# A two-block transformer kernel: expert rows gathered one by one, each with its own wait and its index from the routing's tile

## What is computed

```
eidx = i1 * 128 + i2                       # (tokens, 8, 16) chosen experts
g    = softmax(scores of the chosen)
act  = gelu(sum_d x[t, d] * u[eidx][d])
out[t] = sum over the 128 chosen of g * act * v[eidx]
```

## The kernel before, in words

| block | window in the trace, us | goal | issued before | issued after |
|---|---|---|---|---|
| project, half 1 | 767 to 1024 | 140 | 144 | 156 |
| scan | to 1182 | 200 | 208 | 216 |
| merge | to 1541 | 372 | 384 | 388 |
| norm of the expert layer | to 1580 | 384 | 400 | 400 |
| route | to 1845 | 512 | 512 | 512 |
| final norm, half 0 (next 512 slots) | to 1877 | 10 | 16 | 26 |
| norm of layer two | to 1916 | 24 | 32 | 40 |
| project_two | to 2062 | 110 | 112 | 126 |
| latent_heads | to 2167 | 154 | 160 | 170 |
| attend | to 2389 | 262 | 272 | 278 |
| merge_two | to 2510 | 326 | 336 | 342 |
| norm_add | to 2549 | 338 | 352 | 354 |
| norm of the MLP | to 2589 | 354 | 368 | 370 |
| mlp | to 2869 | 512 | 512 | 512 |

## Time and profile before

### The profile page before, as it was taken

How to read it: one execution, slowest core, us unless ns; L and a number is a source line. 1 busy time by engine, 2 the same in 40 slices (tenths; PEclk the granted TensorE clock), 3 DMA queues, 4 the chain that set the end, 5 groups by cost and what they waited for, 6 DMA issues and landing times. The chain is left out here.

```text
span 3440.3 us, 27636 instructions
## 1 busy us (share of the span) xinstructions
PE 2261.2 (66%) x8920; PEld 1658.5 (48%) x8920; DVE 1935.4 (56%) x3625; ACT 486.0 (14%) x1247; POOL 1348.0 (39%) x1232
## 2 busy tenths in 40 slices
PE   7976999808865488765462642134507993988898
PEld 5745887706625376644321531012306642755763
DVE  3327011588969758655997577685946664061100
ACT  3412100203212100001011001011011101131210
POOL 0000000007765676643565767685746752000000
PEclk9988999859988699887786876555758996979899
DMA  4311443309996799986787987788978996102443
GB/s 137 136 50 32 152 147 122 116 29 403 403 349 230 238 403 378 367 312 215 277 285 243 385 316 255 243 284 283 366 270 325 400 409 245 64 4 100 150 147 116
DMA packets 277281, 807.51 MB, mean 235 GB/s; under 512 B 21024, under 2 KB 37504, under 8 KB 277168
## 3 DMA queue, kind: packets, MB, share of 16 engines
q0 software_dynamic: 149264, 541.41, 42.8%
q1 hardware_dynamic: 127904, 264.69, 21.5%
HBM read 803.92 MB, written 2.10 MB: 234 GB/s over the span
## 5 line engine op out<-in xcount | busy, mean ns | idle before, releaser
L1020 POOL DMA_INDIRECT expert_rows<-in_peer_u,index x512 | 658.1, 1285 | 190.7 <-issue 144.1
L1076 DVE SCALAR_TENSOR_TENSOR expert_rows<-expert_rows,u 128x1024 f32<-128x1024 f32 x512 | 617.3, 1228 | 182.9 <-DMA expert_rows<-in_peer_u,index 151.5
L1020 POOL DMA_INDIRECT expert_rows<-in_peer_v,index x512 | 571.1, 1115 | 191.3 <-issue 146.5
L1089 DVE SCALAR_TENSOR_TENSOR h<-expert_rows,coef,h 128x1024 f32<-128x1024 f32 x224 | 288.2, 1287 | 70.0 <-DMA expert_rows<-in_peer_v,index 51.3
L1089 DVE SCALAR_TENSOR_TENSOR u<-expert_rows,coef,u 128x1024 f32<-128x1024 f32 x220 | 283.3, 1288 | 50.1 <-DMA expert_rows<-in_peer_v,index 48.9
L534 PE MATMUL product<-uT,in_slab 128*128 128x272 f32 (+1 forms) x1024 | 247.1, 398 | 97.1 <-DMA in_slab<-in_w_in 97.1
L1014 POOL COPY index<-chosen 128x8 int32 (+1 forms) x128 | 88.7, 693 | 480.2 <-DVE u L1089 221.2
L2225 PE MATMUL mlp_up<-mlp_xT,mlp_slab 128*128 128x256 f32 x1024 | 230.8, 389 | 48.4 <-ACTq L2242 25.6
L534 PEld LDWEIGHTS product<-uT,in_slab 128*128 128x128 f32 x1024 | 197.8, 197 | 131.7 <-DMA in_slab<-in_w_in 98.1
L2225 PEld LDWEIGHTS mlp_up<-mlp_xT,mlp_slab 128*128 128x128 f32 x1024 | 199.9, 196 | 79.2 <-ACTq L2242 26.0
L2235 PE MATMUL mlp_down<-mlp_slab,upT 128*128 128x512 f32 x512 | 221.3, 593 | 4.2 <-DMA mlp_slab<-in_w_down 4.2
(11 more groups left out here) (377 smaller groups left out, 3264.8 us busy)
## 6 DMA issues: line engine op xcount, KB each, us to landing
in_slab<-in_w_in SPq DMA_DIRECT2D x34, 2048.0 KB, 7.8
mix_slab<-in_w_in SPq DMA_DIRECT2D x20, 2048.0 KB
mlp_slab<-in_w_up SPq DMA_DIRECT2D x16, 2048.0 KB, 8.7
mlp_slab<-in_w_down SPq DMA_DIRECT2D x16, 2048.0 KB, 7.8
mix_slab<-in_ssd_w_out SPq DMA_DIRECT2D x8, 2048.0 KB
q_slab<-in_peer_w_q SPq DMA_DIRECT2D x8, 2048.0 KB, 9.1
mix_slab<-in_sc_w_out SPq DMA_DIRECT2D x4, 2048.0 KB
mix_slab<-in_w_o SPq DMA_DIRECT2D x4, 2048.0 KB
```

Source lines behind the costliest of these rows:

```text
L1020: pool.indirect_dma_start(out=self.rows[b][:], out_offset=None, in_=self.tables[table], in_offset=bass.IndirectOffsetOnAxis(ap=self.index[ ...
L1076: dve.scalar_tensor_tensor(row, row, 1.0, self.u[:, m, :], ALU.mult, ALU.mult, accum_out=self.dots[:, m, ds(column, 1)]).then_inc(self.row ...
L1089: dve.scalar_tensor_tensor(o, row, self.coef[:, m, ds(column, 1)], o, ALU.mult, ALU.add).then_inc(self.rows_used, 1)
```

## The change

The tiles `index` and the copies to them are gone; each gather reads its column of the routing's tile `chosen` itself. The gathers are written out one after the other instead of looping over sixteen, and each waits for the one use of its own tile (by VectorE's count, or by TensorE's for an odd slot of the last 64). The number issued by a block's end is `goal` + 16 and no longer rounded down. VectorE's uses are written out too, with no loops; the instructions themselves and their order are the same. The initial count of 16 in `rows_used` is dropped, and the waits with it.

```diff
-    RING, PART = 16, 8
+    RING = 16
...
-        self.index = [sbuf(ctx, f"index{i}", [P, self.PART], I32) for i in range(self.RING // self.PART)]
...
     def counted(self, n):
 
-        return self.RING + n - max(n - self.shared, 0) // 2
+        return n - max(n - self.shared, 0) // 2
 
     def plan(self, n):
 
@@ -991,103 +990,89 @@
 
     def gather(self, pool, most=None):
 
-        if self.sent == 0:
-            pool.sem_inc(self.rows_used, self.RING)
-        end = min(self.goal + self.RING, self.all) // self.RING * self.RING
+        end = min(self.goal + self.RING, self.all)
         if most is not None:
             end = min(end, self.sent + most)
-        while self.sent < end:
-            table = self.sent // (TT * SLOTS)
-            stop = min(end, (table + 1) * TT * SLOTS)
-            late = self.shared + self.RING
-            if self.sent < late:
-                stop = min(stop, late)
-            per = self.RING if self.sent < late else self.RING // 2
-            first, at = self.sent, self.sent % (TT * SLOTS)
-            with pool.Fori(0, (stop - first) // self.RING) as i:
-                for part in range(self.RING // self.PART):
-
-                    used = first + part * self.PART + self.PART - self.RING
-                    pool.wait_ge(self.rows_used, i * per + self.counted(used))
-                    if self.sent >= late:
-                        pool.wait_ge(self.pe_used, i * per + (used - self.shared) // 2)
-                    pool.tensor_copy(self.index[part][:], self.picks[:, ds(i * self.RING + (at + part * self.PART), self.PART)]
-                                     ).then_inc(self.index_ready, 1)
-                    pool.wait_ge(self.index_ready, i * (self.RING // self.PART) + (first // self.PART + part + 1))
-                    pool.sem_inc(self.index_taken, 1)
-                    for s in range(self.PART):
-                        b = part * self.PART + s
-                        pool.indirect_dma_start(
-                            out=self.rows[b][:], out_offset=None, in_=self.tables[table],
-                            in_offset=bass.IndirectOffsetOnAxis(ap=self.index[part][:, s:s + 1], axis=0)
-                            ).then_inc(self.landed[b], 16)
-            self.sent = stop
+        for n in range(self.sent, end):
+            table, at = divmod(n, TT * SLOTS)
+            s, before = n % self.RING, n - self.RING
+            if before >= self.shared and before % 2:
+                pool.wait_ge(self.pe_used, (before - self.shared) // 2 + 1)
+            elif before >= 0:
+                pool.wait_ge(self.rows_used, self.counted(before + 1))
+            pool.indirect_dma_start(
+                out=self.rows[s][:], out_offset=None, in_=self.tables[table],
+                in_offset=bass.IndirectOffsetOnAxis(ap=self.picks[:, at:at + 1], axis=0)
+                ).then_inc(self.landed[s], 16)
+        self.sent = max(self.sent, end)
...
     def use(self, dve, n):
 
-        end = min(self.done + n, self.goal)
-        while self.done < end:
-            section = self.done // SLOTS
+        for n in range(self.done, min(self.done + n, self.goal)):
+            section, at = divmod(n, SLOTS)
             dot, m = section < TT, section % TT
-            stop = min(end, (section + 1) * SLOTS)
-            if not dot and self.done % SLOTS == 0:
+            if not dot and at == 0:
                 dve.wait_ge(self.gelu_ready, m + 1)
                 dve.tensor_tensor(self.coef[:, m, :], self.gelu[:, m, :], self.weight[:, m, :],
                                   ALU.mult).then_inc(self.coef_ready, 1)
                 dve.wait_ge(self.coef_ready, m + 1)
-                stop = self.done + 2
-            loops = (stop - self.done) // self.RING
-            if loops > 1:
-                with dve.Fori(0, loops) as i:
-                    for s in range(self.RING):
-                        self._one(dve, dot, m, self.done + s, i, in_loop=True)
-                self.done += loops * self.RING
-            else:
-                for n in range(self.done, stop):
-                    self._one(dve, dot, m, n, 0)
-                self.done = stop
+            if dot:
+                self._dot(dve, m, n)
+            elif n < self.shared:
+                self._add(dve, m, n)
+            elif n % 2 == 0:
+                self._add_even(dve, m, n)
+            self.done = n + 1
             if not dot and self.done % SLOTS == 0:
-                dve.wait_ge(self.rows_used, self.counted(self.done))
-                dve.tensor_tensor(self.h[:, m, :], self.h[:, m, :], self.u[:, m, :], ALU.add
-                                  ).then_inc(self.summed, 1)
-                dve.wait_ge(self.summed, m + 1)
-                if self.done > self.shared:
-                    dve.wait_ge(self.pe_used, self.SHARE // 2)
-                    for side in range(2):
-                        o = self.h[:, m, side * 512:(side + 1) * 512]
-                        dve.tensor_tensor(o, o, self.total[side][:], ALU.add)
...
+    def _dot(self, dve, m, n):
+
+        s, at = n % self.RING, n % SLOTS
+        dve.wait_ge(self.landed[s], 16 * (n // self.RING + 1))
+        row = self.rows[s][:]
+        dve.scalar_tensor_tensor(row, row, 1.0, self.u[:, m, :], ALU.mult, ALU.mult,
+                                 accum_out=self.dots[:, m, at:at + 1]).then_inc(self.rows_used, 1)
+
+    def _add(self, dve, m, n):
+
+        s, at = n % self.RING, n % SLOTS
+        o = (self.u if n % 2 else self.h)[:, m, :]
+        dve.wait_ge(self.landed[s], 16 * (n // self.RING + 1))
+        dve.wait_ge(self.rows_used, n - 1)
...
+    def _sum_up(self, dve, m):
...
```

More of the change, by code:

```diff
@@ L1029, in activate @@
             m = self.active
-            act.wait_ge(self.rows_used, self.RING + (m + 1) * SLOTS)
+            act.wait_ge(self.rows_used, (m + 1) * SLOTS)
             act.activation(self.gelu[:, m, :], self.dots[:, m, :], ACT.Gelu).then_inc(self.gelu_ready, 1)
@@ L1068, in _one @@
-    def _one(self, dve, dot, m, n, i, in_loop=False):
-        s = n % self.RING
-        if n >= self.shared and n % 2:
-            return
-        dve.wait_ge(self.landed[s], i * 16 + (n // self.RING + 1) * 16)
-        row, column = self.rows[s][:], i * self.RING + n % SLOTS
-        if dot:
-            dve.scalar_tensor_tensor(row, row, 1.0, self.u[:, m, :], ALU.mult, ALU.mult,
-                                     accum_out=self.dots[:, m, ds(column, 1)]).then_inc(self.rows_used, 1)
-        elif n >= self.shared:
-            o = self.h[:, m, :]
-            dve.wait_ge(self.rows_used, i * (self.RING // 2) + self.counted(n))
-            dve.scalar_tensor_tensor(o, row, self.coef[:, m, ds(column, 1)], o, ALU.mult,
-                                     ALU.add).then_inc(self.rows_used, 1)
-        else:
-            o = (self.u if n % 2 else self.h)[:, m, :]
-            dve.wait_ge(self.rows_used, i * self.RING + (n + self.RING - 1))
-            if n % SLOTS == 1 and not in_loop:
-                dve.tensor_scalar(o, row, self.coef[:, m, 1:2], None, ALU.mult).then_inc(self.rows_used, 1)
-            else:
-                dve.scalar_tensor_tensor(o, row, self.coef[:, m, ds(column, 1)], o, ALU.mult,
-                                         ALU.add).then_inc(self.rows_used, 1)
@@ new lines, in _add @@
+    def _add(self, dve, m, n):
[3 more added lines that the diff above has]
+        dve.wait_ge(self.rows_used, n - 1)
+        if at == 1:
+            dve.tensor_scalar(o, self.rows[s][:], self.coef[:, m, 1:2], None, ALU.mult).then_inc(self.rows_used, 1)
+        else:
+            dve.scalar_tensor_tensor(o, self.rows[s][:], self.coef[:, m, at:at + 1], o, ALU.mult,
+                                     ALU.add).then_inc(self.rows_used, 1)
@@ new lines, in _add_even @@
+    def _add_even(self, dve, m, n):
+        s, at = n % self.RING, n % SLOTS
+        o = self.h[:, m, :]
+        dve.wait_ge(self.landed[s], 16 * (n // self.RING + 1))
+        dve.wait_ge(self.rows_used, self.counted(n))
+        dve.scalar_tensor_tensor(o, self.rows[s][:], self.coef[:, m, at:at + 1], o, ALU.mult,
+                                 ALU.add).then_inc(self.rows_used, 1)
+    def _sum_up(self, dve, m):
+        dve.wait_ge(self.rows_used, self.counted(self.done))
+        dve.tensor_tensor(self.h[:, m, :], self.h[:, m, :], self.u[:, m, :], ALU.add).then_inc(self.summed, 1)
+        dve.wait_ge(self.summed, m + 1)
+        if self.done > self.shared:
+            dve.wait_ge(self.pe_used, self.SHARE // 2)
+            for side in range(2):
+                o = self.h[:, m, side * 512:(side + 1) * 512]
+                dve.tensor_tensor(o, o, self.total[side][:], ALU.add)
```

5 lines of the change are left out of this document (3 added, 2 removed).

## The result

The changed kernel took 3573.31 us (median of four runs, 3561.22 to 3578.82) against 3443.66 for the kernel before (3438.72 to 3451.44): a ratio of 1.037 [1.034, 1.039], slower. In a later group of runs on one chip the same file took 3418.08 against 3447.91, a ratio of 0.992 [0.988, 0.995], slightly faster. Both are results of this kernel; most of what follows is about the 155 us between them.

The account below looks back on a forecast made before the run. Making gathers on GpSimd bounded attend, DMA or VectorE other blocks, with stalls at borders and waits for eight uses. Block terms summed to -58 us: 3440.3 to 3382, plus 7.7 from span to median, gave 3390, range 3343 to 3430.

Parts of the forecast that it names:

- the term of mlp: mlp: first gather about 6 us sooner and 2 rows fewer moved; -9 us (-14 to -2).
- project_two: Block project_two: more gathers, against copy steps saved and more rows in hand; -1 us (-6 to +4).
- The one for slower: Rival: a gather with its own wait always starts 0.81 us behind the last, not 0.30; +97, 3545 us; chance 0.06.
- merge_two's -7: Block merge_two: tail of the part of eight and the drain go behind ScalarE's own end; -7 us (-10 to -3).
- project: Block project: 12 gathers more before the border with the DMA full; +11 us (+6 to +16).
- final norm: Block final norm: 26 gathers for 16 with nothing else going on; +12 us (+10 to +15).
- norm of the expert layer: That norm's block: last use to border falls from 18.9 to 7.7 us; -10 us (-12 to -7).
- merge: Block merge: 16 rows in hand for 8, DMA works through most of the 9.6 us wait; -12 us (-22 to 0).
- latent_heads: Block latent_heads: fewer gathers and copy steps, partly lost to bursts; -3 us (-9 to +7).
- attend: Block attend: 14 copy steps and four gathers fewer, 4 us taken off for bursts; -18 us (-28 to -5).
- the burst rival: Rival: dots run in bursts and each gather beside them costs 2.29 us, taking the gain back; -22, 3426 us; chance 0.15.
- In exchange every block starts with 16 rows in hand: Block ends: last use to border takes 7.7 us; in return blocks start with 16 rows instead of 2 to 16.

Follow-up runs that it names:

- after_again: The changed kernel itself, unaltered, run again as control of a later group; 3418.08 us, ratio 0.992.
- eight_in_mlp_again: The changed kernel with block ends rounded down to sixteen and waits for eight rows at once in mlp only, run again; 3370.42 us, ratio 0.978.
- after: The changed kernel as profiled with the first result; 3573.31 us, ratio 1.037 against the kernel before.
- ends_rounded: The changed kernel with only the rounding of a block's last gather down to a multiple of sixteen put back; 3517.32 us, ratio 1.018.
- parts_of_eight: The changed kernel with GpSimd waiting once for eight rows again, ends not rounded; 3485.73 us, ratio 1.010.
- eight_in_two_third: The changed kernel with ends rounded and waits of eight in mlp and in project_two's main loop; 3397.03 us, ratio 0.985.
- tiny_rows_third: The changed kernel with mlp's gathers cut to 16 columns and its adds to 8; 3575.77 us.
- spaced: As ends_rounded, but in mlp GpSimd makes a small copy and waits for it ahead of each gather; 3407.04 us, ratio 0.988.

## Why the prediction was wrong

The prediction was 3390 us, 3343 to 3430, with 0.06 for slower. The group of the first result lies 183 us above it; the group of after_again, at 3418, lies in the range and is 28 above.

**The step that failed is the term of mlp**, "-9 (-14 to -2)". It took for granted that TensorE runs as long as its slabs are there. Without the stall the term is -12.9 (280.0 to 267.1), inside its range. With it, it is +114.6. The same holds for project_two, "-1 (-6 to +4)": +1.0 without and +12.3 with the stall. None of the rivals had TensorE as the engine that loses. The one for slower put the cost into each gather's start, and that was wrong: gathers with a wait of their own start 0.30 us behind the last. That its 3545 us (3538 with merge_two's -7, which its sum leaves out) lie near the 3573 is chance.

Could it have been seen? Not as a size: the trace of before has no steady run of nine gathers with less than 0.5 us between them, because of the copies and the waits of eight. But I wrote that GpSimd would now issue without gaps, and asked only what that does to VectorE and the DMA, not to the third engine in the block.

**The other terms**, taken from after_again, which has no stall; the earlier trace rows against its stretches:
- project +13.5 for +11, final norm +13.3 for +12, norm of the expert layer -6.7 for -10, merge_two -7.2 for -7, route +0.4 for 0, scan +0.6 for -2, norm of layer two -2.9 for -6, norm_add and norm of the MLP -6.8 for -13.
- merge -4.8 for -12, latent_heads +3.0 for -3, attend -8.0 for -18. These are 23 of the 40 us that are missing.
- All thirteen together: -17.5 for -58; the spans differ by 16.2, the medians by 29.8. The sum lies at that of the burst rival (-22), so that 3418 us is inside the range does not bear the forecast out.

In attend the copies went as planned, but the 86 gathers from `u` took 1572 ns each against 1397 in the earlier trace rows, which gives 15 us back. This is the burst rival's mechanism at about two thirds of its size (18 forecast, 3 by the rival, 8 measured); its price for attend ("3 instead of 18") was too dark and mine too bright.

**A sign was wrong in "In exchange every block starts with 16 rows in hand".** The ends are a part of the change by themselves, and with them rounded again the blocks outside mlp took 3092.0 us (eight_in_mlp_again, 3367.0 - 275.0) against 3157.8 in after_again (3424.1 - 266.3). So by these profiled runs the unrounded ends cost 66 us outside mlp (by the medians 3418.08 and 3370.42, with mlp's 8.7 added, 56); under the stall they cost 59 (3181.3 in after, 3122.6 in ends_rounded). I had seen the price in project and final norm, where the last gathers are issued behind the block's last use, but set it against a gain at the next block's start that never came. GpSimd at the end of project, first in after_again, where VectorE's last dot ends at 1016.3 and the border is at 1038.0, then in eight_in_mlp_again, last dot 1017.9, border 1023.8:

```profile
1019.86 0.93 POOL L1003 DMA_INDIRECT expert_rows<-in_peer_u,chosen  x1 [0.30 <-issue]
1021.10 0.94 POOL L1003 DMA_INDIRECT expert_rows<-in_peer_u,chosen  x1 [0.30 <-issue]
1044.41 1.68 POOL L1003 DMA_INDIRECT expert_rows<-in_peer_u,chosen  x1 [22.37 <-DVE expert_rows L1042]
```
```profile
1006.20 0.97 POOL L1005 DMA_INDIRECT expert_rows<-in_peer_u,chosen  x1 [0.30 <-issue]
1025.40 0.93 POOL L1005 DMA_INDIRECT expert_rows<-in_peer_u,chosen  x1 [18.24 <-SPq L695]
```

With the ring filled to its last tile, project waits 16.0 us from the last gather's end to its border, and scan's first gather must wait for scan's first dot, at 1044.41. With the end rounded, project's gathers are done before its last dot, its border comes 5.9 us after that dot, and scan's first gather starts at 1025.40. "Every block starts with 16 rows in hand" means also that every block starts with no tile free.

**What the parts are worth**, all without the stall: direct index and written-out loops -50 us (3394.62 for 3444.29); the wait per row, outside mlp, another -24 (3370.14 beside it), of which scan gives 8, norm_add 9 and merge_two 6; the unrounded ends +48 (3418.08 for 3370.42, though with mlp 9 us shorter for its own waits per row). The rule that the prediction weighed (the Trainium skill, GPSIMD Engine Reference, Key points) says that GpSimd shares its SBUF interfaces with VectorE and contends with instructions of two SBUF inputs. The traces agree only in part; it depends on when the gather starts. Here are a gather and the add that it starts in, first from after_again's mlp, then from the stall in after:

```profile
2670.05 1.75 POOL L1003 DMA_INDIRECT expert_rows<-in_peer_v,chosen  x1 [0.30 <-issue]
2669.70 1.28 DVE L1054 SCALAR_TENSOR_TENSOR u<-expert_rows,coef,u 128x1024 f32<-128x1024 f32 x1 [0.77 <-DMA expert_rows<-in_peer_v,chosen]
```
```profile
2699.59 0.94 POOL L1003 DMA_INDIRECT expert_rows<-in_peer_v,chosen  x1 [0.30 <-issue]
2699.53 1.32 DVE L1054 SCALAR_TENSOR_TENSOR u<-expert_rows,coef,u 128x1024 f32<-128x1024 f32 x1
```

Started 0.35 us into the add, the gather takes 1.75 us; started 0.06 us into it, 0.94. In the stall nearly all gathers start like the second (113 of 119 from 2630 to 2780 us), and so VectorE can be busy 174.07 of 175.8 us with adds of two inputs and GpSimd not be slowed.

**What stays open.** Three of the six groups had the stall (the one of the first result, the first and the fourth) and three had none; the kernel before took 3444 to 3450 us in all. The record has the first, second and fifth group on chip 15, the third on chip 14 and the fourth on chip 3; the group of the first result has no number. If chip 15 is one and the same, it had the stall in the first group and none 17 and 43 minutes later, so that it is a condition and not the chip; the record doesn't say whether the number counts within one machine. Where the stall exists, traffic and VectorE's adds aren't needed. Nor is a wait for each row: parts_of_eight waits for eight rows at once, and has late matmuls in project_two and merge_two, as eight_in_two_third has in project_two. Whether GpSimd's being busy would do without any transfer wasn't seen where the stall exists. The late matmuls lie in steady runs of gathers with a mean interval of 1.25 to 1.52 us, in mlp, project_two, merge and merge_two; those of 1.55 us and more, in project, route and attend, showed none in any group but a single one near the end of attend in three runs (three late ones in eight_in_two_third's mlp, with a mean of 1.68 us, are the other exception). That speaks for the rate, but it is an argument and not a test. What holds TensorE back stays unknown: no run varied how its instructions reach it, and none tested a limit that the granted clock doesn't show, so both stay as rivals.

## What to carry to other kernels

Asking for more from an engine in the background is a change to every engine beside it: after such a change, read TensorE's rows for "issue" before anything else, and repeat the run on another day or chip before you believe a total. Change one thing at a time: a useful part (the direct index with the written-out loops, 50 us) and a harmful one (the unrounded ends, 56 to 66) came in one diff with a third (the wait per row) that was worth 24 us outside mlp and cost 115 us in it wherever the stall existed. And leave tiles free at a border: what is issued behind the last use lengthens this block, and what is in hand can't be issued in the next.

## What the runs showed of the hardware

- TensorE can fall to one matmul per 2.80 us, one weight load half-way, with nothing awaited, be the matmul one of 0.59 or of 1.01 us; gaps on the way there and back are 0.7 and 1.5 us. In mlp the first late one came 16 to 23 us behind the first gather (16.3 in tiny_rows_third, 22.6 in ends_rounded) and the last 19 to 22 us behind the end of the last, also across 16 us in which GpSimd and the DMA did nothing. It came in three of six groups of runs, with gathers of 4096, 2048 and 64 bytes a row alike.
- A gather that waits for a copy on its own engine starts 0.27 us behind it (spaced); the kernel before has 0.81 us there. What makes the difference wasn't taken apart; a second semaphore instruction and the loop's register stand there too.
- A gather started 0.35 us into an add of VectorE took 1.75 us, one started 0.06 us into it 0.94, as alone (after_again and after, mlp).
- A block whose list on GpSimd ends with gathers in flight had its border 6.0 us behind the last gather's end in a norm of the kernel before and 16.0 us in after_again's project, where the DMA was busy throughout (share 1.01). The last packet of the gathers' queue ended 1.3 and 3.0 us ahead of these borders.
